# Two transformer blocks in fp32 parts: another order of steps in FFN, mixers and delta pairs

## The reference

```python
def swiglu(h, w_gate, w_up, w_down):
    return (silu(h @ w_gate) * (h @ w_up)) @ w_down          # 1024 -> 2816 -> 1024

# first block, twice
h = h + 0.5 * rms_norm(swiglu(rms_norm(h, g0), ...), g1)
u = rms_norm(h, g2)
a_b, a_c, a_x, b_u, c_q, c_k, c_v, d_q, d_k, d_v, d_f, gates = split(u @ w_in)
y_a = (a_b * conv3(a_c * a_x)) @ a_w_out                     # short convolution
y_b = silu(layer_norm(conv31(glu(b_u)))) @ b_w_out           # 31 taps
y_c = diff_attention(c_q, c_k, c_v)                          # 4 heads, normalized per head
y_d = forgetting_attention(d_q, d_k, d_v, d_f)               # 8 heads, decay
h = h + rms_norm(sum(sigmoid(gates[i]) * y[i]) @ w_o, g3)
h = h + 0.5 * rms_norm(swiglu(...), g4)

# second block, twice; alpha = 4 ** 0.25
x = layernorm(alpha * x + 0.5 * swiglu(x), g, b)
qa, ka, va, qkv_b, beta, dt, z, gates = split(x @ w_in)
ya = sliding_window_attention(qa, ka, va, bias, sink) @ w_a  # 16 heads, window 128
qb, kb, vb = silu(conv4(qkv_b))                              # q and k to unit length
yb = (rms(gated_delta_rule(qb, kb, vb, g, beta)) * silu(z)) @ w_b   # 8 heads
x = layernorm(alpha * x + (sig(gates_a) * ya + sig(gates_b) * yb) @ w_out, g, b)
x = layernorm(alpha * x + 0.5 * swiglu(x), g, b)
```

## Time and profile before

| | us |
|---|---|
| median of 3 runs (lowest to highest) | 3339.35 (3338.19 to 3339.7) |
| profiled execution | 3333.8 |
| its span | 3332.1 |
| mean granted PE clock | 0.959 |
| block 1, two layers | 0 to about 1549 |
| block 2, two layers | about 1549 to 3332 |

### The profile page before, as it was taken

One profiled execution on the slowest core, in us unless ns is written; L12 is line 12 of the kernel. 1 busy time (PEld: TensorE's weight loads), 2 busy tenths in 40 slices (PEclk: granted clock), 3 DMA queues, 4 the chain that ended last, 5 costly groups with the idle time before them and its releaser, 6 DMA issues.

```text
span 3332.1 us, 59102 instructions
## 1 busy us (share of the span) xinstructions
PE 3070.4 (92%) x22178; PEld 2901.9 (87%) x22178; DVE 1944.3 (58%) x3310; ACT 1341.5 (40%) x2224; POOL 532.0 (16%) x471
## 2 busy tenths in 40 slices
PE   8989999998989999998898978989989998889998
PEld 7989898998989999897797877989979888789897
DVE  4556776555556876554554576466565536654755
ACT  4344454434344454432333534434333345433332
POOL 0000000000000000001103444431010044444300
PEclk9999999999999999998898999999999989999999
DMA  5544444554544445456552321255545422123453
GB/s 207 182 159 153 132 144 168 176 188 148 189 158 154 142 142 171 165 186 150 198 202 102 102 77 54 87 177 181 190 162 200 160 100 89 64 66 138 170 188 127
DMA packets 72442, 495.49 MB, mean 149 GB/s; under 512 B 8064, under 2 KB 8240, under 8 KB 20176
## 3 DMA queue, kind: packets, MB, share of 16 engines
q1 hardware_dynamic: 67824, 471.95, 41.5%
q0 software_dynamic: 4048, 18.59, 2.1%
q10 hardware_dynamic: 272, 0.99, 0.1%
HBM read 487.31 MB, written 4.19 MB: 148 GB/s over the span
## 4 chain that ended last, share of the span: by engine, by line
issue 74%; PE 12%; DVE 6%; POOL 4%; POOLq 2%; DVEq 2%; ACT 1%; DMA 0%; ACTq 0%; SPq 0%
PE psum L1132 4%; POOL weights_low L908 2%; DVE work L2232 1%; PE psum L1346 1%; PE psum L1352 1%; POOL small L867 1%; POOLq L936 1%; PE psum L1242 1%; POOL residual L937 1%; POOLq L866 1%; DVE small L2257 0%; PE psum L1188 0%; DVE work L2318 0%; PE psum L1457 0%; DVEq L2235 0%
## 5 line engine op out<-in xcount | busy, mean ns | idle before, releaser
L1537 ACT ACTIVATE weights_high<-weight_ring 128x2048 fp32r<-128x2048 f32 (+3 forms) x788 | 906.8, 1171 | 1105.0 <-DMA weight_ring<-stream 1097.6
L1862 DVE TENSOR_TENSOR weights_low<-weight_ring,weights_high 128x2048 fp32r<-128x2048 f32 (+6 forms) x532 | 906.6, 1710 | 757.3 <-ACT weights_high L1537 753.8
L1044 PE MATMUL psum<-normed_t_high,weights_high 128*128 128x256 f32 x2816 | 802.5, 285 | 11.6 <-DVE normed_t_low L1871 10.5
L1044 PE MATMUL psum<-normed_t_low,weights_high 128*128 128x256 f32 x2816 | 800.2, 284 | 0.0
L1044 PE MATMUL psum<-normed_t_high,weights_low 128*128 128x256 f32 x2816 | 799.6, 284 | 0.0
L1044 PEld LDWEIGHTS psum<-normed_t_high,weights_high 128*128 128x128 f32 x2816 | 542.9, 193 | 17.4 <-DVE normed_t_low L1871 11.8
L1044 PEld LDWEIGHTS psum<-normed_t_low,weights_high 128*128 128x128 f32 x2816 | 543.9, 193 | 3.6
L1044 PEld LDWEIGHTS psum<-normed_t_high,weights_low 128*128 128x128 f32 x2816 | 543.6, 193 | 0.0
L1101 PE MATMUL psum<-weights_high,work_parts 128*128 128x512 f32 x1472 | 464.5, 397 | 19.5 <-DVE work_parts L1871 19.5
L1132 PE MATMUL psum<-normed_t_high,weights_high 128*128 128x256 f32 x1248 | 394.8, 316 | 3.2 <-DVE normed_t_low L1871 2.1
L908 POOL TENSOR_TENSOR weights_low<-weight_ring,weights_high 128x512 fp32r<-128x512 f32 (+1 forms) x216 | 346.2, 1618 | 274.6 <-ACT weights_high L1537 274.6
(11 more groups left out here) (268 smaller groups left out, 4477.5 us busy)
## 6 DMA issues: line engine op xcount, KB each, us to landing
weight_ring<-stream SPq DMA_DIRECT2D x400, 1024.0 KB, 4.9
weight_ring<-stream SPq DMA_DIRECT2D x64, 768.0 KB, 4.2
feature_rows<-feat POOLq DMA_DIRECT2D x6, 1024.0 KB, 5.1
work<-toeplitz_rows POOLq DMA_DIRECT2D x8, 512.0 KB, 6.6
feature_rows<-feat POOLq DMA_DIRECT2D x6, 512.0 KB, 3.8
toeplitz_rows<-work POOLq DMA_DIRECT2D x1, 3072.0 KB, 36.4
params<-prms POOLq DMA_DIRECT2D x5, 251.5 KB, 3.3
residual<-x SPq DMA_DIRECT2D x2, 512.0 KB, 4.3
```

Of the source, the lines that this page charges most:

```text
L1044: ins = pe.matmul(PS[:, bank, at:at + S], w[a][:, first + k, c * P:(c + 1) * P], src[b][:, k, :], start=(k, m) == (0, 0), stop=(k, m) == ( ...
L1537: return act.activation(dst, src, ACT.Copy, scale=scale)
L1862: dve.tensor_tensor(some(LOW, i, q, n), some(RING, i, q, n), some(HIGH, i, q, n).bitcast(F32), ALU.subtract).then_inc(low_by_vector, n)
```

## The change

1. `plan_ffn` puts the last but one row product behind the last gate and up. The block-1 and block-2 `wo` products move behind the gates: wo 0 behind gate 29, the other three behind gate 31 (in block 2 the 6th and the last).
2. `affine` moves from POOL to DVE, cut into four pieces of 128 x 512 (two additions or products each): behind units 4, 6, 8 and 10 of an FFN, behind `pk`, both `pq` and `pv` in the mixer. `feature` comes at unit 12. `post2` no longer waits for it. DVE waits once for POOL's memset of g and b ahead of the bias row in block 2's prologue.
3. Block 1's mixer: the dense order is dq, dk, pa, conva, dv instead of dq, dk, dv, pa, conva. Branch c's `out_norm` is split: `out_square` (ACT, POOL), two steps of branch d, `out_norm` (DVE), one step, `out_turn`.
4. Block 2's mixer: `cumg` moves from ahead of the first score into the attention chain; the next pair's three convolutions come first in a pair and the gate behind them; the two heads' `prepare` steps are interleaved and put in at every fourth place; the last two (`dkk`) stand behind `du4`; the DVE scaling of `du4` is a step of its own, `dsc`, behind them.
5. `taps` becomes three steps `tap` and one `taps`, of one operation each; `interleave` lets two waiting items go per chain item while more than four are waiting.

```diff
-        if j >= 2 and j % 2 == 0:
+        if 2 <= j < FB - 2 and j % 2 == 0:
             down(j // 2 - 1)
...
+    down(FP - 2)
     down(FP - 1)
...
-        if later:
-            later.pop(0)()
+        for _ in range(2 if len(later) > 4 else 1):
+            if later:
+                later.pop(0)()
...
-    chain += chain_d[:8]
+    chain += [squares] + chain_d[:2] + [out_norm] + chain_d[2:3] + [(2, out_turn("c"))] + chain_d[3:8]
...
-    dense = [(16, lambda what=what, p=p: project(what, p)) for what in ("dq", "dk", "dv") for p in range(2)]
+    dense = [(16, lambda what=what, p=p: project(what, p)) for what in ("dq", "dk") for p in range(2)]
     dense += [(16, lambda p=p: gate_a(p)) for p in range(4)] + [(16, lambda p=p: value_a(p)) for p in range(2)]
+    dense += [(16, lambda p=p: project("dv", p)) for p in range(2)]
...
-    pl.steps += [gate(24)[0], gate(25)[0]]
+    pl.steps += [gate(j)[0] for j in range(24, 28)]
     acc = pl.step("acc", ("acc", 1), banks=acc_hi, s=1)
...
+    pl.steps += [gate(j)[0] for j in range(28, 30)]
+    wo(0)
+    pl.steps += [gate(j)[0] for j in range(30, 32)]
+    for k in range(1, 4):
+        wo(k)
...
+    beside = [("affine", [("residual_ready", 1)], {"j": (4, 6, 8, 10)}),
+              ("feature", [("feature_rows_loaded", 16)], {"j": (12,)})]
...
+        for h, b in zip(hs, banks):
+            add(h, "dtr", b, [("qk_squares_summed", 1), ("qk_rsqrt_ready", 1)])
+            add(h, "dte", [], [("head_scalars_ready", 1)])
+        for h, b in zip(hs, banks):
+            add(h, "ddc", [3], [("decay_ready", 1), ("strict_decay_ready", 1)])
+            add(h, "dtf", b)
+        for h in hs:
+            add(h, "dkk", [3], [("level_masked", 1)])
...
-    extra = [[(16, lambda: gate(0, 0, "lo3"))] + [(16, lambda w=w: conv(2, w)) for w in range(3)],
-             [(16, lambda: gate(0, 1, "lo3"))] + [(16, lambda w=w: conv(3, w)) for w in range(3)],
+    extra = [[(16, lambda w=w: conv(2, w)) for w in range(3)] + [(16, lambda: gate(0, 1, "lo3"))],
+             [(16, lambda w=w: conv(3, w)) for w in range(3)] + [(16, lambda: gated(2))],
...
-            for n, f in enumerate(todo):
-                chain.insert(2 + 3 * n, (2, f))
+            ends = chain[-4:]
+            chain = chain[:-4]
+            for n, item in enumerate(todo[:8]):
+                chain.insert(2 + 4 * n, item)
+            chain += todo[8:] + ends
...
+            def affine(st):
+
+                if st.p == 0:
+                    dve.wait_ge(feature_rows_loaded, reach("feature_rows_loaded", 16 * st.s))
+                t, cols = st.p // 2, slice(st.p % 2 * HALF, (st.p % 2 + 1) * HALF)
+                dve.tensor_tensor(H[:, t, cols], XN[:, t, cols], PG[:, 0, cols], ALU.mult)
+                dve.drain()
+                dve.tensor_tensor(H[:, t, cols], H[:, t, cols], PG[:, 1, cols], ALU.add).then_inc(residual_ready, 1)
+                dve.drain()
...
+            dve.wait_ge(zeros_set, 3)
```

More of the change, by code:

```diff
@@ L403, in plan_second @@
         pl.steps.append(query(p)[0])
+        affine(1, 1 + p)
     pl.step("pv", "pv", banks=["lo"], unit=("w", 5))
[L405 to L406 removed]
+    affine(1, 3)
     def attention():
@@ L477, in solve @@
         both("du4", [("out_squares_summed", 1), ("out_rsqrt_ready", 1)])
+        for h in hs:
+            steps.append(lambda h=h: pl.step("dsc", ("dsc", h), h=h))
         both("dot", [("delta_out_ready", 1)])
```

177 lines of the change are left out of this document (81 added, 96 removed).

## The result

The changed kernel takes 3285.77 us (median of 4 runs, 3283.40 to 3290.97) against 3338.77 for the one before, measured again beside it. The ratio is 0.9847, with a 95% interval of 0.983 to 0.9864: 53 us or 1.5% faster. The forecast was 3233, a gain of 106, with a range that ends at 3280. The direction was right, the size twice too large.

What follows compares the result with a forecast made beforehand. PE was taken to bound the kernel, busy 3070.4 of 3332.1 us, so only its waits and clock could give time. The parts, 21.9 + 24.3 + 5 + 54.8, sum to 106 us: 3339.35 to 3233, range 3208 to 3280.

Steps and rivals of the forecast that it cites:

- Part 1: Last row products of FFNs and `wo`: work put behind the last gates covers PE's waits, 18.5 us, 21.9 with clock.
- Part 2: First block's mixer: two PE stalls per layer go, 6.9 + 8.0 + 12.4 of clock, minus 3 for new waits: 24.3 us.
- Rival (iv): First mixer: stalls move to `out_turn` and dv's low part, 12 us more than allowed plus 6 of clock: 3251; chance 0.06.
- Part 3: Second residual moved to VectorE: PE's wait in block 2's prologue falls 5 us; VectorE's added work costs PE nothing.
- Part 4 (a): Block 2's mixer, convolutions first in a pair: waits ahead of the pairs' transposes shrink, 14.8 + 0.3 us a layer with clock.
- (c): Block 2's delta pairs, single taps: half of 27.4 us of small waits goes, 6.8 us a layer.
- (b): Block 2's mixer, two heads' decay matrices interleaved: the 2.65 us wait goes, 4.9 us a layer with clock.
- (d): Block 2's first score, `cumg` out of its way: POOL's split blocks the score's small step instead, 0.6 us a layer gained.
- The clock: PE's slow windows behind removed waits regain clock, so PE busy falls some 28 us.
- (i): Block 2's first score also gets free of POOL's split: 14 us more, 3219; chance 0.16.
- (iii): Slower: VectorE work between level products and updates in the pairs, deciding from about 0.9 us per update: 3351; chance 0.10.
- (ii): Pairs' dependent chain: two taps popped per chain item take back (c) and half of (a) and (b), 33 us: 3266; chance 0.16.

Runs made afterwards that it cites:

- experiment 1: The kernel before with only the last but one row product of every FFN moved behind the last gate and up: ratio 0.9942 to the kernel before.
- experiment 2: The changed kernel with the first block's mixer as before (dense order, branch c's squares, scaling and turn together): ratio 0.9873 to the kernel before.
- experiments 3 and 4: Changed kernel, first mixer: dense order conva 0, dv 0, conva 1, dv 1 (0.984 to before); or branch b's taps kept away from branch a's convolution steps (0.9824).
- experiment 10: The changed kernel with the second residual (`affine`) on POOL again and the norm waiting for it: ratio 0.9882 to the kernel before, span 3287.9 us.
- all fourteen kernels: The kernel before, the changed kernel and the twelve experiment kernels; ten have `affine` on VectorE, four have it on POOL.
- experiment 7: The kernel before with only single-operation taps and two waiting items per chain item while more than four wait: ratio 0.9962 to the kernel before.
- experiment 9: The changed kernel with the gate first in the first two pairs and the convolutions behind it: ratio 0.9872 to the kernel before.
- experiment 6: The changed kernel with the scaling `dsc` right behind `du4`, ahead of the next pair's masks: ratio 0.9828 to the kernel before, span 3279.1 us.
- experiment 5: The changed kernel with the second head's scalars behind the first head's decays and their transposes: ratio 0.9829 to the kernel before, span 3274.2 us.
- experiment 8: The changed kernel with taps in blocks of four again and one waiting item per chain item: ratio 0.9925 to the kernel before, span 3304.2 us.

## Why the prediction was half right

*Part 1.* Right in every wait: 18.5 us. "Nothing is added" was wrong by 3 us of layer norm (experiment 1; the VectorE split that used to lie in PE's wait and now stands ahead of the norm's sums is read from the trace).

*Part 2* is the first step that failed. Both old stalls went as priced, but the new waits, "from nothing to 3.5 us a layer, I take 1.5", are 7.1 a layer: 4.7 at dv, the place that the prediction named, 0.5 and 0.6 at the gates, and 1.3 at branch b's norm, which experiment 2 shows to be no work of the order. The turn of branch c, the other place that it named, has no wait at all. The upper end was taken from the stall removed and not from the queue. The row for that was there: VectorE busy 6.46 of 6.70 us in the first window of the earlier trace rows. A stage in which VectorE is full has no cover to give, and experiments 3 and 4 show it: another order moves the wait, less work removes it. Rival (iv) is what happened here by its size, 14.2 us for the 3 allowed, through dv's low part alone. Its half of the clock is not settled: the window behind dv's wait has 0.55, but from 372 to 420 us the granted clock is 1.00 (0.86 before the change).

*Part 3.* The 5 us are right (5.7; experiment 10 gives 3.8 in the wait and 4.6 in the span, and over all fourteen kernels the two means differ by 4.5). The wait on the memset, costed at nothing behind the transfer, costs PE 2.0 us at its first transposes; by the ledger the two stand as -5.7 and +2.0. The Trainium skill, "SBUF — State Buffer", section "Who interferes with whom", says that a VectorE instruction with two inputs in SBUF contends with a GpSimd instruction that reads SBUF. The trace agrees: of the four pieces in each mixer's head, two have a multiplication of 4.9 to 5.0 us instead of 0.69, beside POOL's splits. The prediction allowed for all four and took the cost for PE as 0, and PE has no such wait there.

```profile
1772.34 4.77 POOL L939 TENSOR_TENSOR weights_low<-weight_ring,weights_high 128x2048 fp32r<-128x2048 f32 x1 [10.77 <-ACT weights_high L1554]
...
1772.71 4.95 DVE L2162 TENSOR_TENSOR residual<-work,feature_rows 128x512 f32<-128x512 f32 x1
```

*Part 4 (a)* was right in its own term, 22.0 of 21.8 us. *(c)* was right too for the edit alone in its own waits, 10.2 of 13.6, though 5.6 came back at the transposes (experiment 7). Their sum was wrong: in (a) VectorE's work leaves PE's wait, and nobody then asks where it goes; (c) was worked out from waits in which that work was not yet. Experiment 9 puts a number on it: of 19.7 us won at the transposes 12.0 are given back at the level products. The small waits miss their forecast by 19 us of the 57 missing, more than any other row of waits. The 12.0 are the larger part of it, and 5.6 are at the scaled results, which part 4 put behind the masks without a price (experiment 6: the order moves them, and some 3 really go). *(b)* failed in its sign. It took the interleaving of two heads for distance, and didn't follow VectorE's queue: the second head's scalars, which wait for POOL, were put ahead of the first head's decays (6.1 us a layer, experiment 5). *(d)* was right in its mechanism, with 1.9 for two layers against 1.2. The score's own small step is blocked instead, just as forecast, by POOL's split that starts at 1787.20:

```profile
1787.48 4.25 DVE L2065 TENSOR_SCALAR small<-small 128x2 f32<-128x2 f32 x1
```

The ledger's row has 2.5 more, a wait for a high part next to the score (L1298 before) that is gone and that nobody priced.

*The clock.* The forecast gave back all of it with the waits, and charged none to what is new. It is half: 12.4 of 28, and the windows behind the new waits hold about as much as the rest, which is not shown to be the cause.

*The rivals.* (i) did not come: the score still waits 3.7. (iii) needed 0.9 us per update and got a total of 4 us; (ii) named the right place for the loss with the wrong cause. Of the signs that would have shown the forecast wrong none came up except PE's busy time: the list had no line for dv's low part or for the decays. The measured 3285.77 lies above the range's 3280, since the range left out the case that all unknown costs come together: each was bounded by a stall of its own stage and none by how full VectorE's queue was.

What stays open: why single taps are worth 21 us of span in the new order and 12 in the old. The waits that moved in experiment 8 are listed there, and none of them was tested by itself.

## What to carry to other kernels

When a wait is removed, write down the work of the other engines that ran during it: it has to go somewhere, and where that engine is busy nine tenths of the time, as VectorE was in the first mixer, it goes ahead of the next thing that is waited for. Price a new wait by the queue ahead of it, not by the stall that it replaces, and charge the clock behind it as well. When two dependent chains are interleaved, check for every engine that no step which waits stands ahead of the other chain's step that could run.

## What the runs showed of the hardware

PE's clock behind a wait of 2 us in the delta pairs was 0.78 once (1972.40) and 0.72 once (2043.90), and behind two others of the same length it stayed at full speed (1986.6 to 1994 and 2031.2 to 2038, granted clock 1.00). So waits of equal length do not cost the same, and a sum of the waits alone doesn't give the busy time: in one execution each, the kernel of experiment 2 waits 207.7 us in all and has PE busy for 3066.8, the changed one 211.6 and 3058.0.
